# Local attention inside the first projection: two pieces after every feature block, instead of inside the mixing stage

## The reference, cut to what matters

```
proj = h @ w_in
(aq, ak, av, ag, rq, rk, rv, rg, gq, gk, gv, gg, ga) = jnp.split(proj, IN_SPLITS, axis=-1)
aq, ak, rq, rk = rotary of each
a_out = sliding_window_attention(aq, ak, av, sinks) * jax.nn.silu(ag)      # 8 heads, window 128
r_out = rms_norm(retention(rq, rk, rv)) * jax.nn.silu(rg)                  # 4 heads
g_out = rms_norm(gated_linear_attention(gq, gk, gv, log_a)) * jax.nn.silu(gg)   # 4 heads
y = jnp.concatenate([a_out, r_out, g_out], axis=-1) @ w_out
return x + gate * rms_norm(y, post_gain)
```

## Time and profile before

| what | us |
|---|---|
| time, median of 3 runs | 2092.64 (2091.52 to 2093.15) |
| span of the profiled execution | 2085.9 |
| median time less that span | 6.7 |
| TensorE busy in the span | 1982.1 (95%) |
| VectorE busy | 1089.9 (52%) |
| ScalarE busy | 933.0 (45%) |

### The profile page before, as it was taken

How to read it: one execution, slowest core, us unless ns; L and a number is a source line. 1 busy time by engine, 2 the same in 40 slices (tenths; PEclk the granted TensorE clock), 3 DMA queues, 4 the chain that set the end, 5 groups by cost and what they waited for, 6 DMA issues and landing times.

```text
span 2085.9 us, 25306 instructions
## 1 busy us (share of the span) xinstructions
PE 1982.1 (95%) x9881; PEld 1482.8 (71%) x9881; DVE 1089.9 (52%) x2023; ACT 933.0 (45%) x1737; POOL 12.7 (1%) x28
## 2 busy tenths in 40 slices
PE   8999889999889999889999999999999999999997
PEld 3876446777456888566788888777666668888885
DVE  5623964622874322757655543442386575555333
ACT  3733764643664333574432222344587443223223
POOL 1000000000000000000000000000000000000000
PEclk8999999999989999999999999999999999999999
DMA  8331432223203433003233333425400123333331
GB/s 289 118 92 51 162 101 81 71 71 83 81 21 87 147 92 92 8 2 116 74 98 101 92 93 100 110 54 125 146 2 2 51 71 101 101 92 99 94 95 47
DMA packets 301267, 183.13 MB, mean 88 GB/s; under 512 B 17550, under 2 KB 292108, under 8 KB 299948
## 3 DMA queue, kind: packets, MB, share of 16 engines
q1 hardware_dynamic: 295437, 166.05, 27.6%
q10 hardware_dynamic: 4704, 13.31, 1.7%
q0 software_dynamic: 1008, 2.15, 0.3%
HBM read 179.22 MB, written 2.27 MB: 87 GB/s over the span
## 4 chain that ended last, share of the span: by engine, by line
PE 85%; DVE 8%; ACT 4%; issue 1%; DMA 1%; ACTq 0%; DVEq 0%; SPq 0%
PE PS L911 22%; PE PS L913 22%; PE PS L912 22%; PE PS L1057 3%; PE PS L1085 3%; PE PS L1070 2%; PE PS L1211 1%; DVE WLO L2088 1%; ACT WHI L1523 1%; PE PS L1234 1%; PE PS L1243 1%; DVE X L2055 1%; PE PS L1129 1%; PE PS L1150 1%; PE PS L1138 1%
## 5 line engine op out<-in xcount | busy, mean ns | idle before, releaser
L912 PE MATMUL PS<-LO,WHI 128*128 128x512 f32 x1690 | 660.3, 391 | 0.0
L911 PE MATMUL PS<-HI,WHI 128*128 128x512 f32 x1578 | 626.5, 397 | 26.5 <-DVE LO L2061 9.2
L913 PE MATMUL PS<-HI,WLO 128*128 128x512 f32 x1578 | 617.0, 391 | 0.0
L2088 DVE TENSOR_TENSOR WLO<-RING,WHI 128x1024 fp32r<-128x1024 f32 (+3 forms) x271 | 314.4, 1161 | 532.6 <-ACT WHI L1523 531.6
L1523 ACT ACTIVATE WHI<-RING 128x1024 fp32r<-128x1024 f32 (+3 forms) x271 | 272.6, 1007 | 471.9 <-PE PS L913 450.1
L911 PEld LDWEIGHTS PS<-HI,WHI 128*128 128x128 f32 x1578 | 297.8, 189 | 109.4 <-issue 27.2
L912 PEld LDWEIGHTS PS<-LO,WHI 128*128 128x128 f32 x1690 | 319.0, 189 | 64.8 <-issue 1.2
L913 PEld LDWEIGHTS PS<-HI,WLO 128*128 128x128 f32 x1578 | 297.7, 189 | 63.2
L911 PE MATMUL PS<-HIDDEN,WHI 128*128 128x512 f32 x352 | 137.1, 389 | 0.6 <-PE PS L913 0.6
L912 PE MATMUL PS<-HIDDEN,WHI 128*128 128x512 f32 x352 | 137.0, 389 | 0.0
L913 PE MATMUL PS<-HIDDEN,WLO 128*128 128x512 f32 x352 | 136.9, 389 | 0.0
(11 more groups left out here) (346 smaller groups left out, 2355.8 us busy)
## 6 DMA issues: line engine op xcount, KB each, us to landing
RING<-in_ffn_w_up SPq DMA_DIRECT2D x88, 512.0 KB, 3.8
RING<-in_w_in SPq DMA_DIRECT2D x48, 512.0 KB, 3.9
RING<-in_w_mod SPq DMA_DIRECT2D x32, 512.0 KB, 4.6
RING<-in_ffn_w_down SPq DMA_DIRECT2D x32, 512.0 KB, 4.0
RING<-in_ev_w_in SPq DMA_DIRECT2D x30, 512.0 KB, 3.9
RING<-in_w_out SPq DMA_DIRECT2D x16, 512.0 KB, 4.6
RING<-in_od_w_in SPq DMA_DIRECT2D x15, 512.0 KB, 4.0
RING<-in_ffn_w_down SPq DMA_DIRECT2D x16, 384.0 KB, 3.4
```

Source lines behind the costliest of these rows:

```text
L911: mm(bank, WHI[i2][:, i, :], hi, start=(k == 0), stop=False)
L912: mm(bank, WHI[i2][:, i, :], lo, start=False, stop=False)
L913: return mm(bank, WLO[i2][:, i, :], hi, start=False, stop=last)
L2088: tt(WLO[i2][:, 0:nk, :], raw, WHI[i2][:, 0:nk, :], ALU.subtract).then_inc(me.signals(w_split), 1)
```

## The change

The local attention no longer runs in `mix` but inside `proj` of the same layer. `with_window` walks through the jobs and gives out 20 slots (`WINDOW_SLOTS`): after the seventh feature block one, then two for each block, one in the middle of its 24 products (`beside`) and one behind it (a job of kind W), the last behind the gate block G. In a slot i the lane does `scores(i)`, `turn(i - 3)` and `values(i - 4)` on TensorE, `scaled(i - 1)` and `recips(i - 2)` on VectorE, `exps(i - 1)`, `normalise(i - 2)`, `mixed(i - 4)` and `collect(i - 3)` on ScalarE. It uses PSUM banks 4 to 7. The block of `av` is made earlier so that the values are there. `mix` keeps the other two mixers; the four gate products of the local attention (`gated`) move from its end to between two `masked` steps, and the order of splitting at its end changes. The exponentials' table is loaded once more, in `proj`. Buffers move, the scores are now exponentiated in place in four buffers.

```diff
+        PAIR_S = S.rearrange("p a t -> p (a t)")[:, 0:2056].rearrange("p (r a t) -> p r a t", r=4, a=2)
+        PAIR_ET = E.rearrange("p a t -> p (a t)")[:, 0:1024].rearrange("p (r a b q) -> p r a b q", r=2, a=2, b=2)
...
+            jobs += turned_jobs([feat(w, 640, src, z(AV))])
...
+            jobs += [feat(w, 768, src, z(AG), how="silu", first=True)]
+            jobs += [feat(w, 768 + 128 * i, src, z(AG + i), how="silu") for i in range(1, 4)]
             jobs += [feat(w, 2048 + 128 * i, src, z(RG + i), how="silu") for i in range(2)]
             jobs += [feat(w, 2816 + 128 * i, src, z(GG + i), how="silu") for i in range(2)]
-            return woven(jobs)
+            return with_window(woven(jobs))
+
+        def with_window(jobs):
+
+            got, slots, n_feature = [], WINDOW_SLOTS, 0
+            for j in jobs:
+                n_feature += j["kind"] == "F"
+                got.append(j)
+                if j["kind"] == "F" and n_feature > FIRST_BESIDE and slots:
+                    j["beside"], slots = True, slots - 1
+                if j["kind"] == "G" or j["kind"] == "F" and n_feature >= FIRST_BESIDE and slots:
+                    got.append(dict(kind="W", chunks=[]))
+                    slots -= 1
+            return got
...
-        MIX_SLOTS = 18
+        WINDOW_SLOTS, FIRST_BESIDE = 20, 7
...
+                    if j["kind"] == "W":
+                        next(lane)
+                        continue
...
+                                if k == total // 2 and j.get("beside"):
+                                    next(lane)
...
-                scores(0)
-                yield
-                for i in range(MIX_SLOTS):
-                    if i + 1 < len(todo):
-                        scores(i + 1)
-                    if 0 <= i - 1 < len(todo):
-                        turn(i - 1)
-                    if i >= 2:
-                        values(i - 2)
+                for i in range(WINDOW_SLOTS):
+                    if i < len(todo):
+                        scores(i)
+                    if 0 <= i - 3 < len(todo):
+                        turn(i - 3)
+                    if i >= 4:
+                        values(i - 4)
                     yield
...
-                window, state = swa_lane(l), state_lane(l)
-                next(window)
-                next(state)
-                for _ in range(MIX_SLOTS):
-                    next(window)
-                    next(state)
-                for _ in state:
+                for _ in state_lane(l):
                     pass
...
+                               lane=swa_lane(l) if s == "proj" else None)
...
+                for i in range(WINDOW_SLOTS):
+                    if i == 1:
+                        act.preload_act_table_set(LN_EXP)
                     if 0 <= i - 1 < len(todo):
+                        exps(i - 1)
+                    if 0 <= i - 2 < len(todo):
+                        normalise(i - 2)
+                    if i >= 4:
+                        mixed(i - 4)
+                    if 0 <= i - 3 < len(todo):
+                        collect(i - 3)
                     yield
...
...
-                act.wait_ge(gla_near, NB * (l + 1) - 1)
-                inputs(inputs_of("out")[0:3], True)
-                act.wait_ge(gla_near, NB * (l + 1))
+                inputs(inputs_of("out")[0:4], True)
                 weights(at_split[0] + 2)
                 act.preload_act_table_set(LN_EXP)
+                act.wait_ge(gla_near, NB * (l + 1))
+                inputs(inputs_of("out")[4:6], True, 4)
                 gla_mix(NB - 1)
                 gla_squares(l)
-                inputs(inputs_of("out")[3:6], True, 3)
                 gla_rstd(l)
                 inputs(inputs_of("out")[6:8], True, 6)
                 yield
...
+                for i in range(WINDOW_SLOTS):
+                    if 0 <= i - 1 < len(todo):
+                        scaled(i - 1)
+                    if 0 <= i - 2 < len(todo):
+                        recips(i - 2)
...
+                def gated(k):
+                    tt(H[:, k, :], z(AQ + k), z(AG + k), ALU.mult).then_inc(me.signals(normed), 1)
...
                 masked(4)
+                gated(0)
+                gated(1)
                 masked(5)
+                gated(2)
+                gated(3)
...
-                weigh(NB - 1)
-                weights(at_split[0] + 1)
-                low(0, H[:, 0, :], None)
-                weights(at_split[0] + 2)
-                if len(GROUPS[l]) > 1:
-                    modulated(1)
-                for k in (1, 2):
-                    low(k, H[:, k, :], None)
-                gated(3)
                 for _ in range(2):
                     me.emptied_by("act")
                 dve.wait_ge(*me.last)
                 rstd_known()
                 for t in range(2):
                     tt(H[:, 4 + t, :], z(RG + t), RET_RS[:, t, :], ALU.mult).then_inc(me.signals(normed), 1)
-                for k in (3, 4, 5):
+                weigh(NB - 1)
+                for k in range(4):
+                    low(k, H[:, k, :], None)
+                weights(at_split[0] + 1)
+                if len(GROUPS[l]) > 1:
+                    modulated(1)
+                weights(at_split[0] + 2)
+                for k in (4, 5):
                     low(k, H[:, k, :], None)
                 dve.wait_ge(gla_mixed, NB * (l + 1))
                 for t in range(2):
```

143 lines of the change are left out of this document (63 added, 80 removed).

## The result

The changed kernel takes 2117.47 us (median of 4, 2115.02 to 2120.46) against 2092.08 of the kernel before (4 runs beside it): a ratio of 1.0131, 95% interval 1.0115 to 1.0147. It is 25.4 us slower, where the forecast was +7.0 and its range ended at 2108. The span of the profiled execution is 2118.6.

A forecast was written before the change was run, and what follows sets the result against it. TensorE bounds the projection; the mixing is bound by VectorE and chains across engines. Projections +57.2 us, mixings -50.2, together +7.0: span 2092.9, time 2099.6, range 2089 to 2108; the sums' bounds allowed -11 to +22.

The forecast's parts named there:

- the price of a piece: In proj on TensorE: attention's matmuls cost 1.76 us a two-block pair, 0.97 a one-block pair, 24.5 taken a layer.
- the term of the loops: In the mixing's three GLA rounds: each loop falls to 37.1 us, 12.5 less in layer 0, 14.9 in layer 1.
- the clock rival: In mixing and start of out: thinned TensorE work runs more often at 1.2 GHz, +12 to +14, about 2106; chance 0.17.
- lower end of 21.1: In proj: attention's TensorE cost a layer in us, if all pieces scale by the value block's transposes, 0.49 / 0.58.
- the rival on the faster side: In proj: pieces at the value block's price and no waits, 42.2 us in all, giving 2084.6; chance 0.14.
- ScalarE's lateness: In proj at rotated blocks eight to ten: TensorE waits for ScalarE 1.9 + 1.1 + 1.1 = 4.1 us a layer.
- The fronts: In the mixing up to the end of the first products_within: 38.8 to 30.1 us, 8.7 less in each layer.
- the replay: In the mixing's front: new order written out with rows' durations and 0.1 us per hand-over, gates pushing decays to 14.7.
- by the same replay the next `near_sums` comes 1.5 us late: In layer 0's loop: seven w_mod steps together on TensorE delay near_sums 1.5 us, hidden by the next round's exponents.
- a loop exceeds 39: Sign of being wrong: a mixing loop over 39 us because TensorE at the lower clock becomes late for weigh.
- The tails: In the mixing after the last products_within: 20.6 for 23.2 us in layer 0, 13.4 for 16.2 in layer 1.
- The rival without a stall: In proj: ScalarE's lateness is swallowed, 25 us a layer, 50 against 50.2, giving 2092.4, no change; chance 0.21.

The follow-up runs named there:

- e15: Kernel after without attention, with matmuls of the attention's own shapes on constants in each of 20 slots: projection 165.8 us, 2.00 us a slot, one run.
- e13: Kernel after without attention, with four 128x128 transposes that wait for nothing in each slot: projection 134.8 us, 0.45 us a slot, one run.
- e14: Kernel after without attention, with eight 128x128 transposes in each slot: projection 143.4 us, 0.88 us a slot, one run.
- e12: Kernel after with ScalarE's copy of the turned scores first in its slot, turning and values in their old slots: ratio 1.0101 to before.
- e4: Kernel after with turning and values one slot later (21 slots) and ScalarE's copy of the turned scores first in its slot: ratio 1.0080 to before.
- e5: Kernel after with the mixing's end in its old order and the four gate products back at the end: ratio 1.0112 to before.
- e3: Kernel after with the first five w_mod steps of layer 0's mixing moved earlier, into TensorE's waits in the front: 2111.67 us, ratio 1.0096 to before.
- e2: Kernel before with the local attention left out of the mixing, everything else in its order: 2040.95 us, ratio 0.9760 to before.

## Why the prediction was wrong

The step that failed is the price of a piece on TensorE in the projection's sum; the term of the loops failed beside it. The direction held, the size did not, and the clock rival's 2106 was nearer for other reasons than its own.

- **The price of a piece** is the term most mis-sized: 24.5 us a layer forecast, 30.3 measured, and 26 had been set as its upper end. The mixing's rows were the right ones (two-block pair 1.76 forecast, 1.81 measured), but they were counted 16 times from start to start, where 20 slots have a way in and out (together 0.19 each); and one-block pairs, halved to 0.97, cost 1.15 (0.42 + 0.36 + 0.37). 12 x 1.81 + 4 x 1.15 + 20 x 0.19 = 30.1. e15 shows that this price needs no wait. Scaling by the value block's transposes gave a lower end of 21.1 that none of the slots measured with the attention's shapes comes near, and with it went the rival on the faster side. e13 and e14 measure 108 ns for a transpose of 128 columns in the stream. The Trainium skill (TensorE: Matmul & The Clock Gate, "Wait — 56ns, not 53.3ns?") gives start to start as columns over 2.4 GHz plus 2.5 ns, 56 ns here. The page's series is of bf16 matmuls, these transposes are float32, and they take about twice that; so the forecast was right to give that price no weight.
- **ScalarE's lateness** was right: 4.1 forecast, 4.25 and 4.26 measured, in slots 3, 5 and 7 and behind `normalise` or `collect`, split 1.2, 1.8, 1.2 and not 1.9, 1.1, 1.1. e12 and e4 confirm its cause.
- **The fronts** gave 7.6 each for 8.7: 31.2 for 30.1. `decays` starts 15.3 us in, where the replay had 14.7. The gates do what was counted: beside e5, whose front without them takes 30.0, the first two fill a wait (it falls from 2.34 to 1.14) and the other two push `decays` back by 1.2.
- **The loops.** VectorE's work was right to 0.4 us, and the first round too (12.7 for 12.3). In layer 0 the failing step is "by the same replay the next `near_sums` comes 1.5 us late, which `exponents` of the next round hides". It ended 7.7 us into the second round, and VectorE waited 4.5 us behind it, by way of ScalarE's copy and the exponentials that stand behind that in its queue. The load of the sixteenth step and the lower clock behind it made it so late; e3, with the steps moved, has 13.5 for 17.35. In layer 1 the third round takes 13.3: four far products at the lower clock take 3.3 us, and VectorE waits 0.6. The mark "a loop exceeds 39" was met in layer 0, with the clock as the smaller part of the cause.
- **The tails** came out as computed, 20.3 and 13.9 for 20.6 and 13.4, but a part of the change works against them. e5's 19.2 and 12.4 show that the new order costs 1.1 and 1.5. (The old chain of the forecast adds up to 6.4 from its own terms, not to the 6.6 written there.)
- **The clock** cost 1.4 us in layer 0's projection, where I had not looked for it, and 1.6 in the second round of that layer's loop. In the mixing it is as low as the rival said (0.78 in layer 1's loop, 0.83 before), but the fronts and tails are at 0.84 to 0.95 and came out as forecast without it.
- **The range** left out its own upper bound, +22, as unlikely. The pieces (11.6) and the loops (9.1) erred to one side, and with the fronts (2.2) and the clock (1.4) they make nearly all of the 24.8 between the two sums. (The rival without a stall was summed with 25 a layer; with the forecast's own 24.5 it lies 1 us lower.)

## What to carry to other kernels

Small matmuls between long ones should be priced by slot, from the last long product to the next, with the changes of tile shape in them; a row of equal transposes in the same stream is no substitute. When a result comes late in a replay, follow it through the queues of the other engines, in order, before calling it hidden: here late products held up a copy, and the exponentials that VectorE needed stood behind that copy. And work moved from a stage with idle engines into one that TensorE fills must give back more than its full price: here a pair cost 1.6 us in the mixing (50.3 / 32, e2) and 2.2 in the projection (70.6 / 32).

## What was unexpected of the hardware

- Four 128x128 transposes take 0.35 us in front of full products and 0.58 in front of matmuls with 64 output rows (e13, e15); a break in the products with transposes alone costs 0.02 us.
- Equal idle time and equal work lowered the granted clock at one place (0.79) and not at another (1.00), the same way in three traces; in a fourth (e5) it fell behind an earlier wait.
- In two executions of one kernel the same step waited for its load to nearly the same point (13.4 and 13.1 us behind the front), but the granted clock behind it was 0.68 in one and 1.00 in the other, and the round took 17.35 and 15.55 us.
